# One DMA transpose for every row head, and later places for row heads' operations in the first and last attention tiles

## What is computed

```python
def one_chunk(args):                      # 64 queries, 8 heads of 64
    c, qb = args
    kb = lax.dynamic_slice_in_dim(kp, c * CHUNK, BAND, axis=1)     # own chunk and 8 before
    vb = lax.dynamic_slice_in_dim(vp, c * CHUNK, BAND, axis=1)
    s = jnp.einsum('bqhd,bkhd->bhqk', qb, kb).astype(jnp.float32) * scale + bias[None]
    s = jnp.where(valid[None, None, None, :], s, MASK_VALUE)       # keys before position 0
    p = jax.nn.softmax(s, axis=-1)
    return jnp.einsum('bhqk,bkhd->bqhd', p.astype(vb.dtype), vb)
```

## Time and profile before

| | |
|---|---|
| median of three runs | 1647.23 us (1642.43 to 1650.64) |
| the profiled execution | 1641.95 us |
| its span, first to last instruction | 1640.2 us |
| mean granted TensorE clock | 0.993 of full speed |
| PE, DVE, ACT, POOL busy | 96%, 63%, 50%, 41% of the span |
| attention phase | from about 846 us to the end |

### The profile page before, as it was taken

One profiled execution on the slowest core, in us unless ns is written; L12 is line 12 of the kernel. 1 busy time (PEld: TensorE's weight loads), 2 busy tenths in 40 slices (PEclk: granted clock), 3 DMA queues, 4 the chain that ended last, 5 costly groups with the idle time before them and its releaser, 6 DMA issues.

```text
span 1640.2 us, 42712 instructions
## 1 busy us (share of the span) xinstructions
PE 1575.8 (96%) x17344; PEld 1178.5 (72%) x17344; DVE 1036.2 (63%) x2134; ACT 826.0 (50%) x1541; POOL 665.0 (41%) x666
## 2 busy tenths in 40 slices
PE   7999999999999999999987899999999999999976
PEld 3455455468677777767766788998888898888854
DVE  7977867747565566556435566666666666666665
ACT  6655555522121111112125677676776776776774
POOL 2543433311101111111313466556665666655654
PEclk9999999999999999999999999999999999999989
DMA  6556556473514533542764788777778767778664
GB/s 248 214 193 219 195 207 219 179 269 136 218 66 172 201 112 134 180 169 89 219 213 118 173 201 204 183 190 172 190 200 199 196 177 176 191 194 201 162 166 107
DMA packets 296987, 297.37 MB, mean 181 GB/s; under 512 B 169912, under 2 KB 230344, under 8 KB 294744
## 3 DMA queue, kind: packets, MB, share of 16 engines
q1 hardware_dynamic: 296264, 293.99, 61.1%
q0 software_dynamic: 528, 0.66, 0.3%
HBM read 150.87 MB, written 83.54 MB: 143 GB/s over the span
## 4 chain that ended last, share of the span: by engine, by line
PE 60%; SPq 6%; DMA 5%; POOL 4%; ACT 3%; issue 2%; DVE 1%; DVEq 0%; ACTq 0%; POOLq 0%
PE bank L1154 9%; PE bank L1996 6%; PE bank L1130 6%; PE bank L1133 6%; PE bank L1132 6%; DMA stages<-rows 5%; PE bank L1739 4%; PE bank L1742 4%; PE bank L1741 4%; PE bank L1919 3%; SPq L2419 2%; POOL stages L2354 2%; PE bank L2050 2%; PE bank L2052 2%; PE bank L2051 2%
## 5 line engine op out<-in xcount | busy, mean ns | idle before, releaser
L1739 PE MATMUL bank<-middle,weights 128*128 128x128 f16 x1792 | 310.0, 219 | 8.8 <-ACT middle L1749 4.1
L1741 PE MATMUL bank<-middle,weights 128*128 128x128 f16 x1792 | 309.7, 219 | 0.0
L1742 PE MATMUL bank<-middle,weights 128*128 128x128 f16 x1792 | 309.7, 219 | 0.0
L2370 POOL TENSOR_TENSOR rows<-rows 128x640 f16<-128x640 f32 (+4 forms) x128 | 174.1, 1360 | 281.5 <-ACT rows L2173 281.5
L1130 PE MATMUL bank<-middle 128*128 128x256 f16 x784 | 213.7, 273 | 0.5 <-DVE stages L1270 0.5
L1132 PE MATMUL bank<-middle 128*128 128x256 f16 x784 | 213.7, 273 | 0.0
L1133 PE MATMUL bank<-middle 128*128 128x256 f16 x784 | 213.7, 273 | 0.0
L1996 PE MATMUL bank<-entry,stages 128*128 128x512 f16 x768 | 186.0, 379 | 0.7 <-DVE stages L2237 0.7
L1739 PEld LDWEIGHTS bank<-middle,weights 128*128 128x128 f16 x1792 | 175.4, 98 | 11.3 <-issue 4.4
L1741 PEld LDWEIGHTS bank<-middle,weights 128*128 128x128 f16 x1792 | 175.5, 98 | 0.4
L1742 PEld LDWEIGHTS bank<-middle,weights 128*128 128x128 f16 x1792 | 175.4, 98 | 0.0
(11 more groups left out here) (168 smaller groups left out, 3952.3 us busy)
## 6 DMA issues: line engine op xcount, KB each, us to landing
entry<-in_x SPq DMA_DIRECT2D x64, 512.0 KB, 3.7
h_ops<-middle SPq DMA_DIRECT2D x16, 1792.0 KB, 6.1
middle<-h_ops SPq DMA_DIRECT2D x112, 256.0 KB, 5.5
middle<-h_ops SPq DMA_DIRECT2D x49, 512.0 KB, 7.5
residual<-entry SPq DMA_DIRECT2D x32, 512.0 KB, 2.7
middle<-middle SPq DMA_DIRECT2D x128, 128.0 KB, 3.1
out<-entry SPq DMA_DIRECT2D x31, 512.0 KB, 3.1
entry<-residual SPq DMA_DIRECT2D x30, 512.0 KB, 5.4
```

Source lines behind the costliest of these rows:

```text
L1739: nc.tensor.matmul(dst, wh, hop3[:, o, 0, kt, :], start=(kt == 0 and s < 2 and pair == 0), stop=False, skip_group_check=True)
L1741: nc.tensor.matmul(dst, wh, hop3[:, o, 1, kt, :], start=False, stop=False, skip_group_check=True)
L1742: mm = nc.tensor.matmul(dst, wl, hop3[:, o, 0, kt, :], start=False, stop=(kt == 3), skip_group_check=True)
L2370: nc.gpsimd.tensor_tensor(r16[:, j, 1, c:640], r32[:, j, c:640], r16[:, j, 0, c:640], ALU.subtract).then_inc(A["rpl_done"], 1)
```

## The change

Four things are changed. First, tiles 0 and 1 turned a row head with four DMA transposes, one for each j and each part, which left out the key blocks that don't exist; now every row head is turned by one DMA transpose of all 20 blocks, as tiles 2 to 15 were already. For this POOL sets the whole of `r16` to zero once, and a scratch buffer `junk0` moves out of `r16`. Second, the first `turn` is issued at the end of the phase before, ahead of the waits for the residual's stores, and so ahead of the first two loads of output weights. Third, in tiles 0 and 1 the j = 0 part of a row head moves on ACT to the end of the odd head, and on POOL behind the `rstd` and key splits of that head. Fourth, from head 4 of tile 14 to the end (`late_rows`) the j = 1 part of a row head moves on ACT and POOL behind all three groups of the column head. In tiles 1 to 15 the `rstd` of an even head moves on POOL from behind the first group to behind the last (in the late stretch behind the row head's part too).

```diff
@@ buffers
-        junk0 = view(X, 5120, (640,), BF16)
+        junk0 = view(X, 10240, (512,), BF16)
@@ end of q_phase_sp
             for b in range(2):
                 store_res(PBLK * (PTILES - 1) + b + 2)
+            turn(sp, 0, 1)
             for s in range(2):
                 sp.wait_ge(r_stored[s], 16 * 2 * PTILES)
@@
         def turns(heads):
-            return 64 * min(heads, 2 * HALF) + 16 * max(heads - 2 * HALF, 0)
+            return 16 * heads
@@
+        def late_rows(t, h):
+            return t == LAST or (t == LAST - 1 and h >= HALF)
@@ attention_masks, after its wait
+            nc.gpsimd.memset(r16[:, :, :, :], 0.0).then_inc(A["rows_set"], 1)
@@
+        def turn(sp, t, h):
+            head = HEADS * t + h
+            if head == 1:
+                sp.wait_ge(A["rows_set"], 1)
+            sp.wait_ge(A["rpl_done"], row_count(t, h, 1) + 1)
+            at_least(sp, A["pv_mm"], head - 1)
+            sp.dma_start_transpose(pT[:, :, :, :, :].rearrange("p j a i n -> p (j a i) n"),
+                                   r16[:, :, :, :].rearrange("p j a n -> p (j a n)")).then_inc(turned, 16)
@@ the turn of before
-                for j in range(2):
-                    skip = max(0, first_block(t) - j)
-                    for part in range(2):
-                        sp.dma_start_transpose(pT[:, j, part, skip:5, :], r16[:, j, part, skip * P:640]).then_inc(turned, 16)
@@ ACT, head(t, h)
-                    if t2 < ATILES:
+                    if t2 < ATILES and t >= 2:
                         row_exponential(t2, h2, 0)
                 else:
                     exponential(t, h, 2)
-                    row_exponential(t1, h1, 1)
+                    if not late_rows(t, h):
+                        row_exponential(t1, h1, 1)
                     exponential(t, h, 0)
                     other(t, h, 0)
                     exponential(t, h, 1)
+                    if late_rows(t, h):
+                        row_exponential(t1, h1, 1)
@@ end of ACT's head(t, h)
+                if by_rows(h) and t < 2:
+                    row_exponential(t2, h2, 0)
@@ POOL, even heads
                         for k in range(len(groups(t))):
                             p_lo(t, h, k)
                             if early and k == 0:
                                 row_lo(t, h + 1, 1)
-                            if k == 0:
-                                for of, j in finish_at(t, h):
-                                    rstd(of, j)
+                        if late_rows(t, h):
+                            row_lo(t, h + 1, 1)
+                        for of, j in finish_at(t, h):
+                            rstd(of, j)
@@ SPq, tile 0
                     for s in (0, 1):
                         load_hop3(sp, 2, s)
-                    turn(t, 1)
                     load_wob(2)
```

More of the change, by code:

```diff
@@ L1562, in build @@
             bias_k_loaded mask_done fg_loaded wob_hi wob_lo out_mm out_done
-            shift_done rexp_done rph_done rpl_done max_mm max_done mrow_mm mrow_done st_mm bias_done exp_done ph_done pl_done
+            rows_set shift_done rexp_done rph_done rpl_done max_mm max_done mrow_mm mrow_done st_mm bias_done exp_done ph_done pl_done
             pv_mm rc_done ya_done yt_mm yth_done ytl_done ss_done ms_done rstd_done fin_done""".split()
@@ L1966, in maximum @@
             nc.vector.tensor_tensor_reduce(
-                (junk0 if t == 0 and h == 0 else junk2)[:, c:640], wide[:, c:640], bias_q[:, h // 2, c:640], 1.0, -3e38,
+                junk0[:, 0:640 - c] if t == 0 and h == 0 else junk2[:, c:640], wide[:, c:640], bias_q[:, h // 2, c:640], 1.0, -3e38,
                 ALU.add, ALU.max, m16[:, h // 2 % 2, j:j + 1]).then_inc(A["max_done"], 1)
@@ L2375, in a_phase_pool @@
                 for h in range(HEADS):
+                    t2, h2 = ahead(t, h, 2)
                     if by_rows(h):
-                        t2, h2 = ahead(t, h, 2)
                         for of, j in finish_at(t, h):
                             rstd(of, j)
-                        if t2 < ATILES:
+                        if t2 < ATILES and t >= 2:
                             row_lo(t2, h2, 0)
                     else:
-                        early = group_of(t, 2)[0] is not None
-                        if not early:
+                        early = group_of(t, 2)[0] is not None and not late_rows(t, h)
+                        if not early and not late_rows(t, h):
                             row_lo(t, h + 1, 1)
@@ L2389, in a_phase_pool @@
                                 row_lo(t, h + 1, 1)
-                            if k == 0:
-                                for of, j in finish_at(t, h):
-                                    rstd(of, j)
+                        if late_rows(t, h):
+                            row_lo(t, h + 1, 1)
+                        for of, j in finish_at(t, h):
+                            rstd(of, j)
                     if split_at(t, h):
                         kq_lo(pool, split_at(t, h))
+                    if by_rows(h) and t < 2:
+                        row_lo(t2, h2, 0)
             for j in range(2):
@@ L2438, in a_phase_sp @@
                 else:
-                    turn(t, 1)
+                    turn(sp, t, 1)
                     load_v(sp, t, 1)
@@ L2446, in a_phase_sp @@
                 if t == LAST:
-                    turn(t, 3)
+                    turn(sp, t, 3)
                     sp.wait_ge(A["kq_mm"], PRODUCTS * 2 * ATILES)
@@ L2450, in a_phase_sp @@
                         sp.dma_start(res_last[:, j, :], r_dram[2 * LAST + j]).then_inc(last_loaded[j], 16)
-                    turn(t, 5)
-                    turn(t, 7)
+                    turn(sp, t, 5)
+                    turn(sp, t, 7)
                     continue
```

## The result

| | before | after |
|---|---|---|
| median | 1644.18 us (20 runs, 1640.02 to 1650.64) | 1648.06 us (20 runs, 1645.63 to 1651.75) |
| ratio to before, 95% interval | | 1.0022, 1.0013 to 1.0032 |
| span of the profiled execution | 1640.2 us | 1646.0 us |

The change makes the kernel 0.2% slower, by 3.9 us of the medians, where the forecast said 1.6 us: its case of no difference that counts. Under it lie two shifts of 8 and 12 us that nearly cancel.

A forecast was written before the change was run, and what follows sets the result against it. The row ring (transpose, landing, copy) was taken to bound head and tail, PE the middle. -11.4 head, +12 tail, +1 clock gave +1.6 us on 1647.23: 1648.8 us, own range 1642 to 1655, whole range 1637 to 1657.

The forecast's parts named there:

- The head's gain: Tiles 0 and 1: one transpose for four shortens the row ring, 11.4 us gained, bounds 6 and 20.7.
- Sum at head 5: 5.8 us: Tile 0: SPq free 2.5 us sooner, landing 2.4 sooner, 0.9 for head 3's start.
- rival (a): Late landings in the head and a slow clock in the tail: +9, 1656 us; chance 0.20 together with (d).
- The first turn: Start of the head: issued early, it delays two weight loads on SPq by about 0.7 us, 3.15 at worst.
- The tail's loss: End of tile 14 and tile 15: groups 0 and 1 inside the row ring lose 12 us, between 9 and 16.
- Each pay 2.5: Tail: six transposes, tile 14's head 5 to tile 15's head 7, each 2.5 us later, 15.0 us before deductions.
- PE's gain from POOL's earlier low parts: Tail: PE's 8.6 us wait shrinks but moves to the next transpose, so the gain is costed at nothing.
- rstd: Tail and 13 middle tiles: its place behind the groups changes nothing, bounds -1 and +3 us.
- The clock: An allowance of 1 us added to the sum for the granted clock.
- Rival (b): The head gives all, the ring no longer binding in tile 0: about -9.5, 1638 us; chance 0.10.
- (c): Tail: the late rows are hidden and most of the 8.6 us is gained: -20, 1627 us; chance 0.08.
- (d): The change does nothing in the head, transposes being hidden: +12, 1659 us; chance 0.20 together with rival (a).

The follow-up runs named there:

- e2_four: early_two with four small transposes again for row heads of tiles 0 and 1; 1640.08 us, 0.9976 of the kernel before.
- e2_first: early_two with the first turn back behind the first two weight and two operand loads; 1631.02 us, 0.9914 of the kernel before.
- tail_only: Experiment 2: the kernel before with only the late places of the row head and of rstd; 1658.73 us, ratio 1.0085.
- head_only: The changed kernel with the tail's old places of the row heads, rstd staying late; 1639.53 us, 0.9969 of the kernel before.
- after_rstd: The changed kernel with rstd put back behind the first group; 1648.75 us, 1.0038 of the kernel before.
- e2_rstd: early_two with rstd back behind the first group in all tiles; 1628.83 us, 0.9908 of the kernel before.
- (6): early_two with the old places of j = 0 on ACT and POOL in tiles 0 and 1; 1634.21 us, 0.9934 of the kernel before.
- (11): early_two with the edits of e2_first and e2_rstd together, the kernel called best; 1627.86 us, 0.9913 of the kernel before.
- best: early_two with the first turn and rstd both back at their old places; 1627.86 us, 0.9913 of the kernel before.
- early_two: head_only with a second r16 buffer for head 7 of tile 14 and heads 3 and 7 of tile 15; 1632.67 us, 0.9930 of before.

## Why the prediction was right, and where its sizes were off

The forecast of nearly no change came out, by the mechanism given for it: the head gains, the tail loses about as much, and the middle stands. The steps in turn:

- **The head's gain: right in kind, too large.** The term was 11.4 us; tile 2 starts 8.4 us sooner, and `e2_four` puts the one transpose at 7.6. The shortfall is all in tile 0. "Sum at head 5: 5.8 us" was 2.0, and "7.2" at head 7 was 3.6, while the rest, "I take 4.2", measured 8.4 - 3.6 = 4.8. The failing term is the landing of head 3. I counted on SPq being free 2.5 us sooner and on 0.9 us for its start. It started 0.7 sooner, held SPq for 4.45 us and not 3.15, and landed after 8.1 us, later than the 7.5 that I had kept as the bound; the copy behind it came at 871.83, before at 871.18. Of the next two, head 5's took 6.5 and only head 7's, 5.0, was near the 5.1. This is the half of rival (a) that came true, 3 us of its 4.8, though not by the two landings that it named.
- **The first turn: larger than said.** The delay of the weights was put at 0.7 us, 3.15 at worst. The turn's issue took 3.90 us. ACT has the weights 2.0 us later than with the old order, and `e2_first` gets 2.1 back at tile 2.
- **The memset: right.** It takes 2.24 us (2.6 were reckoned) and what follows it on POOL starts 0.3 us late, long ahead of the phase.
- **The tail's loss: right in mechanism, size near.** From the turn of tile 14's head 3 to the start of PE's last row values the stretch went from 1625.92 - 1549.03 = 76.9 us to 1630.42 - 1540.94 = 89.5, 12.6 longer, for the 12 forecast. The step of 10.57 became 13.90 where the sum said 13.1; 0.7 of the difference is the time to the landing, 5.8 for 5.1. "Each pay 2.5" isn't how it is spread, though: the six steps grew by 3.5, 1.8, 0.8, 3.3, 1.6 and 2.6. `tail_only` shows the loss alone (with the late `rstd`), 14.0 us; on top of `head_only` it is 8.7, and with two buffers 7.
- **PE's gain from POOL's earlier low parts: nothing, as said.** The wait for POOL went and waits for the landing, for ACT's queue and for DVE came.
- **rstd: nothing, as said**, by `after_rstd`. The 3.6 us that `e2_rstd` shows once the ring is loosened would be its bound of +3, but they are within the scatter.
- **The clock: +1 was near.** Beyond the 12.6 us the end is another 1.3 us later. PE takes 7.8 us from the start of its last row values to its last product, before 6.5; the granted clock in the two slices of four us from 1628 is 0.73 and 0.84, before 1.00 and 1.00.

The sum by the traces is 12.6 + 1.3 - 8.1 = 5.8 us, as the two spans say; the medians say 3.9, the forecast said 1.6. That the measured median, 1648.06, is within a microsecond of the forecast 1648.8 is luck: the kernel before came out 3.05 us lower over 20 runs than over the three that I started from, and the difference 2.3 larger. Rival (b), that the head gives all, fell with head 3's landing, (c), that the late rows are hidden, with the tail's turns, and (d) with the head's 8 us.

What stays open: why `head_only`'s step of 13.47 us is longer than before's 10.57. Of the 2.9 us, 1.8 are the landing (6.9 us for 5.1), and the same turn lands in 6.7 or 6.8 us in all seven other kernels that change the head and keep the tail's old places, so it isn't chance; why it does, no run shows. Of the rest, in its trace PE waits 2.98 us there for the second half of tile 14's branch, whose first half stands behind the waiting copy on ACT; the second buffer removes the step, but no run moved that branch alone. Nor does a run show how much of the 5.3 us of experiment 2 is the late `rstd`, counted twice. And the j = 0 places (6) and the two edits together (11) are within the scatter.

## What to carry to other kernels

Before an edit of places, write down the ring that leads from a buffer's release back to it, with its length in each stretch: what was put inside here cost near its full length (12.6 us for six times 2.5), and a place changed in the stretch that PE bounds cost nothing that the times can tell. When two parts of a change have opposite signs, time each alone; here 5 us faster and 14 us slower looked like no change at all, and the first part with a second buffer at the bottleneck was 0.7% faster, with old places of `rstd` or of the first turn 0.9%. A landing time is one of its place: take it from a transfer that starts beside the same loads, not from the median of calmer tiles. It can change where nobody changed the transfer: two landings of the tail, 5.0 and 4.9 us before, were 6.8 and 6.4 in `head_only`.

## What was unexpected of the hardware

- The same transpose of 20 blocks landed in 4.9 us in most tiles and in 8.1 us in tile 0, right behind two weight and five operand loads; of that, its issue on the queue was 4.45 us for 3.1. The first turn of `best`, behind two weight and two operand loads, took 9.9. The DMA share in the four us from 863 of the changed kernel was 0.97, in those from 867 0.99; in the kernel before 0.76 and 0.33. With four of the loads behind it the issue was short again and the landing 6.5, at a share of 0.68 and then 0.99; whether what is issued behind a transpose slows it too, no run separates.
- The granted clock was at half speed, 0.50, from 1564 to 1572 us of the changed kernel's tail, after PE's wait of 3.5 us at 1562.84. The kernel before had 1.00 in both of these slices. PE's products are stretched by it: those with row values took 0.24 us each at 1563.16 and 0.19 at 1624.72. The slice from 1568:

```profile
1568.00:1572.00 4.00, 1.38 (x26) 1.23 (x24) 2.15 (x5) 0.18 (x2) 1.70 (x3) 0.50 0.49 94
```

The Trainium skill (TensorE: Matmul & The Clock Gate, HAM oscillation) describes this pattern of bursts and waits. The trace agrees in this place. It wasn't always a single long wait that came first: in `head_only` the slices of four us from 1564, 1568 and 1572 are at 0.50, 0.50 and 0.73, and none of PE's waits from 1556 to 1564.01, where the first stretched product starts, was longer than 1.24 us. In `early_two` they are at 0.68, 0.50 and 0.97, in the changed kernel at 0.50, 0.50 and 0.60.
